# Weight sums of the last product moved from the MLP's first half to the three output projections

## The chip, the cores and the metric

One core of a Trainium2 chip runs the whole kernel. The metric is device time in microseconds (us) of one execution. Three runs of the kernel before gave 1279.53, 1282.16 and 1282.68 us, so the median is 1282.16 us. One further execution was profiled: it took 1281.15 us, of which 1279.1 us lie between its first and its last instruction. Less than 0.3% (3.8 us) is not told from no change here.

## The reference

The reference is one layer of an encoder over two sequences, a prompt of 512 rows and a sample of 256 rows, each with 16 shared meta rows in front. All data are float32, the width is 1024. Cut to its steps:

```
u    = rms(h);  q, kv, k_rot, conv_in, gates = split(u @ w_in)
attn = latent_attention(q, kv, k_rot) @ w_o_attn                  # 8 heads
c    = depthwise_conv31(glu(conv_in)) + b
c    = silu(layernorm(c));  conv = c @ w_conv_out
h    = h + (sig(gA) * attn + sig(gC) * conv) @ w_out
h    = h + square(relu(rms(h) @ w_mlp_in)) @ w_mlp_out            # hidden width 4096
y    = rms(h)[:, 16:]
```

## The kernel before

**Products.** Each float32 product is made of three TensorE products on a high and a low part of each operand (`products`, L359): high by high, high by low, low by high. The high part is a rounded copy (`hi_unit`, L319, always on ScalarE), the low part is the difference between the weights and their high part (`lo_unit`, L324). A *unit* is 128x1024 weights: it lands in one of four `raw` slots, is split into one of two `whi` and one of two `wlo` slots, and is used by 48 matmuls (36 in the token-major `w_out`, L1850). The split of unit n+2 starts when TensorE has finished unit n. In most of the first part VectorE makes the low parts, because GpSimd ("POOL") has other work later; in the three output projections (`w_o_attn`, `w_conv_out`, `w_out`, eight units each) and in the MLP's first half GpSimd makes nearly all of them.

**Seven products instead of eight.** The last product, hidden by `w_mlp_out`, is done as a two by two block product with seven block products (a Strassen form). It needs sums and differences of the four blocks of `w_mlp_out`. They are made once by the kernel: for each of eight parts j, ScalarE issues two loads of 1 MB into a staging slot (`load_sums`, L841), VectorE makes four subtractions of 128x1024 elements in place (`weight_sums`, L1289 to L1295), and ScalarE issues two stores of 1 MB to a scratch tensor `wsum` in HBM (`store_sums`, L846). There are three staging slots; the list `W_SLOT` says which part uses which. The seven products read `wsum` back much later. Before the change, parts 0 and 1 are loaded at the start of `w_out`, part 2 in the middle of it, and parts 3 to 7 are handled in the MLP's first half.

**The stage around the change.** Every engine has its own list of instructions, written out by hand and run strictly in order; semaphores tie them together. TensorE's list for the three output projections is: eight units of `w_o_attn`, eight of `w_conv_out`, four units of `w_out` for the left half of the columns, four for the right half. Between them stand small products with a matrix of ones: after the first unit the column sums for the LayerNorm's mean (L1810), and after unit 4 of `w_o_attn` those for its variance (L1821). For the variance ScalarE squares eight centred tiles (`ln_squares`, L798) and GpSimd adds the squares up one after the other into `lnacc` (`ln_sq_add`, L1525 and L1528), between its low parts of weights. TensorE waits at L1821 until all eight are added, and what follows in its list waits behind it.

In the loop over the eight units m of `w_conv_out`, VectorE multiplies unit m's result with its gate (`gconv`, L1257), adds it to `zacc` (L1260), and after ScalarE's rounded copy `zhi` (L825) makes the low part `zlo` (L1262). ScalarE's list has, for each m, the high part of the weights of unit m+1 and then `zhi` of m. So the weights' high part of unit m+2 stands behind `zhi` of m, and that waits for VectorE's addition of m.

During the right half of `w_out`, TensorE transposes the new rows of `h` (L1857) for the MLP. The first four transposed tiles share one accumulator, so each waits until VectorE has made the low part of the tile before it (`u2_lo`, L1282), and that waits for ScalarE's high part (`u2_hi`, L836). SyncE ("SP") issues the loads of weights (L407, L486), gates (`gin`, L478) and the rows of x into `h1` (L496).

The two lines that make one part's first difference wait and run are:

```
dve.wait_ge(wst_landed[j], 32)
nc.vector.tensor_tensor(out=b11, in0=b12, in1=b11, op=ALU.subtract).then_inc(wst_made, 1)
```

Of the kernel before, what the change touches and what calls it, by code (L numbers as in the profile page):

```python
# [32 lines left out]
F32 = mybir.dt.float32  # L33
# [6 lines left out]
P = 128  # L40
D = 1024
# [49 lines left out]
W_SLOT = (2, 0, 0, 0, 1, 0, 1, 0)  # L91
# [42 lines left out]
def build(nc, t):  # L134
    with ExitStack() as ctx:
# [83 lines left out]
        gconv = at("gconv", [P, TQ], F32, Z0 + 134912)  # L219
# [17 lines left out]
        wst = [[at(f"wst{e}{g}", [P, 2, D], F32, Z0 + o + 8192 * g) for g in range(2)] for e, o in enumerate((90112, 73728, 151552))]  # L237
# [161 lines left out]
        def _(sp):  # L399
# [91 lines left out]
            for g in range(2 * KD + 3):  # L491
                m = g % KD
                if g == 2 * KD:
                    sp.wait_ge(c_lo, KD)
                    for e, (name, t0, nt) in enumerate((("x_prompt", 0, 4), ("x_sample", 4, 2))):
                        sp.dma_start(h1[:, t0:t0 + nt], t[name][0].rearrange("(t p) n -> p t n", p=P)) \  # L496
                          .then_inc(h_landed[e], 16)
# [42 lines left out]
        def _(act):  # L540
# [245 lines left out]

            for h in range(EARLY_HEADS, HEADS):
# [20 lines left out]
            hi_unit(act, U_O, 1, 3)  # L808
            for k in range(KD):
# [27 lines left out]
            wm = t["w_mlp_out"][0].rearrange("(g u k p) n -> g p u k n", g=2, k=2, p=P)  # L837

            def load_sums(j):
                for g in range(2):  # L840
                    act.dma_start(wst[W_SLOT[j]][g][:, :, :], wm[g, :, j]).then_inc(wst_landed[j], 16)  # L841

            def store_sums(j):
                act.wait_ge(wst_made, 4 * (j + 1))
                for g in range(2):
                    act.dma_start(wsum[g, j], wst[W_SLOT[j]][g][:, :, :]).then_inc(wst_stored[j], 16)  # L846
            act.wait_ge(unit_used, U_OUT)
            load_sums(0)
            act.wait_ge(z_lo, KD)
            load_sums(1)  # L850
            hi_unit(act, U_OUT, 0, 1)
            hi_unit(act, U_OUT, 0, 2)
            store_sums(0)
            hi_unit(act, U_OUT, 0, 3)
            store_sums(1)
            hi_unit(act, U_OUT, 0, 4)
            act.wait_ge(wst_stored[1], 32)
            load_sums(2)
            for i in range(NT):
                h_square(0, i)  # L860
            hi_unit(act, U_OUT, 0, 5)
            hi_unit(act, U_OUT, 0, 6)
            act.wait_ge(wst_stored[0], 32)
            store_sums(2)
# [28 lines left out]
            def in_step(i):  # L893
                for c in range(4):
# [54 lines left out]
        def _(dve):  # L949
# [268 lines left out]

            def gate_attn(m):
# [22 lines left out]
            gate_attn(2), gate_attn(3), gate_attn(4)  # L1242
# [11 lines left out]
            for m in range(KD):  # L1254
                dve.wait_ge(unit_used, U_CO + m + 1)
# [24 lines left out]
            def u2_lo(k):  # L1280
                dve.wait_ge(u2hi_ready, k + 1)
                nc.vector.scalar_tensor_tensor(out=u2lo[:, k], in0=psum[:, U2_PAIR[k], 0:TQ], scalar=vcol("norm_mlp", k),  # L1282
                                               in1=u2hi[:, k].bitcast(F32), op0=ALU.mult, op1=ALU.subtract).then_inc(u2lo_ready, 1)
            def weight_sums(j):

                a, b = wst[W_SLOT[j]]
                b11, b12, b21, b22 = a[:, :, 0:HALF], a[:, :, HALF:D], b[:, :, 0:HALF], b[:, :, HALF:D]
                dve.wait_ge(wst_landed[j], 32)
                nc.vector.tensor_tensor(out=b11, in0=b12, in1=b11, op=ALU.subtract).then_inc(wst_made, 1)  # L1289
                dve.wait_ge(wst_made, 4 * j + 1)  # L1290
                nc.vector.tensor_tensor(out=b12, in0=b22, in1=b12, op=ALU.subtract).then_inc(wst_made, 1)
                dve.wait_ge(wst_made, 4 * j + 2)
                nc.vector.tensor_tensor(out=b22, in0=b22, in1=b11, op=ALU.subtract).then_inc(wst_made, 1)
                dve.wait_ge(wst_made, 4 * j + 3)
                nc.vector.tensor_tensor(out=b21, in0=b22, in1=b21, op=ALU.subtract).then_inc(wst_made, 1)  # L1295

            weight_sums(0), weight_sums(1)
            h_add(0)
            weight_sums(2)
# [45 lines left out]
            def in_step(i):  # L1345
                for c in range(4):
# [3 lines left out]
                    if f == KH:  # L1350
                        for j in range(3, PU):
                            dve.wait_ge(wst_stored[j], 32)
# [6 lines left out]
                    if f in (2, 4, 6, 9, 12):  # L1359
                        weight_sums((2, 4, 6, 9, 12).index(f) + 3)  # L1360
# [82 lines left out]
        def _(gp):  # L1443
# [92 lines left out]
            for n in range(U_O + KD, U_IN + 1):  # L1536
# [435 lines left out]
```

## Time and profile before

| | us |
|---|---|
| median of three runs | 1282.16 |
| profiled execution | 1281.15 |
| its span, first to last instruction | 1279.1 |
| TensorE busy with matmuls | 1249.1 |
| VectorE busy | 813.0 |
| ScalarE busy | 486.5 |
| GpSimd busy | 257.0 |
| HBM read, written | 115.32 MB, 26.21 MB |

TensorE's clock was granted in full for 0.996 of the span. A busy share says how full an engine is over all stages; for one stage it has to be read in a window of it. In a list of instructions in order of time, the bracket at a row's end gives the time for which the engine stood idle before that instruction, and what ended that. VectorE's duration of an instruction can contain waiting inside it: the same subtraction of 128x1024 elements shows 1.22 us in some rows and 3.3 us in others.

### The profile page before, as it was taken

To read this page: it belongs to the slowest core of one execution; us is meant where nothing else is said; L and a number is where in the kernel's file an instruction comes from. 1 tells how busy PE (TensorE), PEld (TensorE's weight loads), DVE (VectorE), ACT (ScalarE), POOL (GpSimd) and SP (SyncE) were. 2 spreads that over 40 slices of the span, in tenths; PEclk is the share of its full clock that TensorE was granted. 3 is DMA by queue.
4 is the path that set the end of the run, shared out by engine and by line. 5 is a ranking of instruction groups with operands and counts; after the bars stand their busy time and mean duration, and the time that the engine had idled before them with its cause. 6 is when DMAs were issued, how large, how long until landed. Compare 5 with 4: busy or idle time off the path is not lost.

```text
span 1279.1 us, 17675 instructions
## 1 busy us (share of the span) xinstructions
PE 1249.1 (98%) x7037; PEld 1086.7 (85%) x7037; DVE 813.0 (64%) x966; ACT 486.5 (38%) x731; POOL 257.0 (20%) x172
## 2 busy tenths in 40 slices
PE   6999999999999999989999989999999999999997
PEld 4888888888889999978888878888888888888886
DVE  4699999998867777764833533645111146678865
ACT  6211122532156676753621224221222244444452
POOL 2000000000034344347322322323333210000001
PEclk9999999999999999999999999999999999999999
DMA  6222222333220011114353935665312234333332
GB/s 188 67 66 66 57 67 66 104 111 107 90 66 22 22 42 33 34 30 144 100 203 109 361 141 181 237 224 201 124 55 63 66 111 149 131 126 126 131 132 98
DMA packets 136693, 142.36 MB, mean 111 GB/s; under 512 B 10573, under 2 KB 106891, under 8 KB 134586
## 3 DMA queue, kind: packets, MB, share of 16 engines
q1 hardware_dynamic: 127488, 101.55, 26.3%
q10 hardware_dynamic: 9146, 40.01, 8.2%
q8 instruction: 39, 0.64, 0.2%
q14 instruction: 20, 0.16, 0.0%
HBM read 115.32 MB, written 26.21 MB: 111 GB/s over the span
## 4 chain that ended last, share of the span: by engine, by line
PE 88%; DVE 4%; ACT 3%; DMA 2%; issue 2%; ACTq 1%; POOL 0%; POOLq 0%; DVEq 0%
PE psum L359 59%; PE psum L1929 17%; PE psum L1714 4%; PE psum L1746 2%; PE psum L1850 2%; DMA wst<-in_w_mlp_out 2%; PE psum L1726 1%; PE psum L1672 1%; DVE acc L1030 1%; PE psum L1590 1%; PE psum L1555 1%; DMA wsum<-wst 1%; ACT uhi L565 0%; DVE olo L1178 0%; PE psum L1857 0%
## 5 line engine op out<-in xcount | busy, mean ns | idle before, releaser
L324 POOL TENSOR_TENSOR wlo<-raw,whi 128x1024 fp32r<-128x1024 f32 (+2 forms) x70 | 166.6, 2380 | 684.1 <-ACT whi L319 684.1
L1030 DVE SCALAR_TENSOR_TENSOR acc<-cs,convw,acc 128x799 f32<-128x799 f32 x232 | 230.2, 1057 | 0.2
L319 ACT ACTIVATE whi<-raw 128x1024 fp32r<-128x1024 f32 (+1 forms) x113 | 114.0, 1009 | 294.1 <-PE psum L359 253.6
L359 PE MATMUL psum<-uhi,wlo 128*128 128x512 f32 x592 | 152.8, 339 | 0.0
L359 PE MATMUL psum<-uhi,whi 128*128 128x512 f32 x592 | 152.2, 338 | 0.5 <-DVE wlo L324 0.5
L359 PE MATMUL psum<-ulo,whi 128*128 128x512 f32 x592 | 152.5, 338 | 0.0
L1355 DVE SCALAR_TENSOR_TENSOR hid<-psum,rbc 128x768 f32<-128x768 f32 x32 | 30.6, 956 | 174.0 <-PE psum L359 173.9
L359 PE MATMUL psum<-u2hi,whi 128*128 128x512 f32 (+1 forms) x512 | 131.0, 336 | 0.0
L359 PE MATMUL psum<-u2hi,wlo 128*128 128x512 f32 (+1 forms) x512 | 130.6, 336 | 0.0
L359 PE MATMUL psum<-u2lo,whi 128*128 128x512 f32 (+1 forms) x512 | 130.6, 336 | 0.0
L916 ACT ACTIVATE hid<-hid 128x768 f32<-128x768 f32 x32 | 27.1, 846 | 200.5 <-DVE hid L1355 182.8
L359 PEld LDWEIGHTS psum<-uhi,whi 128*128 128x128 f32 x592 | 91.4, 188 | 14.0 <-issue 0.8
L359 PEld LDWEIGHTS psum<-uhi,wlo 128*128 128x128 f32 x592 | 91.6, 188 | 12.9
L359 PEld LDWEIGHTS psum<-ulo,whi 128*128 128x128 f32 x592 | 91.3, 188 | 12.3
L886 ACT ACTIVATE hidhi<-hid 128x768 fp32r<-128x768 f32 x56 | 47.3, 846 | 110.2 <-PE psum L1929 108.9
L359 PEld LDWEIGHTS psum<-u2lo,whi 128*128 128x128 f32 x512 | 78.3, 188 | 10.5
L359 PEld LDWEIGHTS psum<-u2hi,whi 128*128 128x128 f32 x512 | 78.3, 188 | 10.3
L359 PEld LDWEIGHTS psum<-u2hi,wlo 128*128 128x128 f32 x512 | 78.1, 188 | 10.5
L1329 DVE TENSOR_TENSOR hidlo<-hid,hidhi 128x768 fp32r<-128x768 f32 x56 | 53.7, 960 | 50.9 <-ACT hidhi L886 50.9
L324 DVE TENSOR_TENSOR wlo<-raw,whi 128x1024 fp32r<-128x1024 f32 (+1 forms) x39 | 47.1, 1207 | 30.2 <-ACT whi L319 30.2
L1929 PE MATMUL psum<-whi,hidlo 128*128 128x512 f32 x168 | 65.4, 389 | 0.0
L1929 PE MATMUL psum<-wlo,hidhi 128*128 128x512 f32 x168 | 65.4, 389 | 0.0
(243 smaller groups left out, 2512.7 us busy)
## 6 DMA issues: line engine op xcount, KB each, us to landing
raw<-in_w_in SPq DMA_DIRECT2D x38, 512.0 KB, 4.0
wst<-in_w_mlp_out ACTq DMA_DIRECT2D x16, 1024.0 KB, 8.0
wsum<-wst ACTq DMA_DIRECT2D x16, 1024.0 KB, 5.9
raw<-in_w_mlp_in SPq DMA_DIRECT2D x32, 512.0 KB, 4.0
raw<-wsum SPq DMA_DIRECT2D x32, 512.0 KB, 4.1
raw<-in_w_mlp_out SPq DMA_DIRECT2D x24, 512.0 KB, 3.6
gates<-gout ACTq DMA_DIRECT2D x16, 384.0 KB, 2.5
gin<-gates SPq DMA_DIRECT2D x16, 384.0 KB, 3.1
```

What stands on the lines that cost most here:

```text
L319: nc.scalar.activation(whi[:, c % 2, 0:w], raw[:, c % 4, 0:w], ACT.Copy).then_inc(hi_ready, 1)
L324: eng.tensor_tensor(out=wlo[:, c % 2, 0:w], in0=raw[:, c % 4, 0:w], in1=whi[:, c % 2, 0:w].bitcast(F32), op=ALU.subtract).then_inc(lo_read ...
L359: mm = nc.tensor.matmul(out[:, o0:o0 + n], a, b[:, k, c0:c0 + n], start=first and step == 0, stop=last and step == 2)
L886: nc.scalar.activation(hidhi[u % 4][:, :, :], f_block(n, c), ACT.Copy).then_inc(hidhi_ready, 1)
L916: nc.scalar.activation(r, r, ACT.Square).then_inc(hid_ready, 1)
L1030: ins = nc.vector.scalar_tensor_tensor(out=a, in0=src, scalar=w, in1=a, op0=ALU.mult, op1=ALU.add)
L1329: nc.vector.tensor_tensor(out=hidlo[u % 4][:, :, :], in0=f_block(n, c), in1=hidhi[u % 4][:, :, :].bitcast(F32), op=ALU.subtract).then_inc( ...
L1355: nc.vector.scalar_tensor_tensor(out=hid[:, ds(i * 4 + c, 1), :], in0=psum[:, pair:pair + 1, 0:TQ], scalar=0.0, in1=rbc[:, :].rearrange("p ...
L1714: mm = nc.tensor.matmul(psum[:, q % 2, e * HALF:e * HALF + n], a[:, c0:c0 + P], b[:, grp["k0"] + k0:grp["k0"] + k0 + n], start=step == 0, ...
L1746: mm = nc.tensor.matmul(bank[:, 7, 0:2 * P], a[:, vt, hh * VD:(hh + 1) * VD], r[:, blk % 2, e, :], start=e == 0 and step == 0, stop=False)
L1850: mm = nc.tensor.matmul(out, a, b[:, kk, :], start=first and step == 0, stop=last and step == 2)
L1929: mm = nc.tensor.matmul(bank[:, P_BANKS[n % 2][tt]], a, b[:, kk, :], start=c == 0 and kk == 0 and step == 0, stop=c == PU - 1 and kk == 1 ...
```

## The change

All eight parts of the weight sums are made during the three output projections, none in the MLP's first half. There are now five staging places instead of three, in memory that is free at the time, and `W_SLOT` names them anew. Four things move:

1. Parts 0 and 1 are loaded at the end of attention and at the start of `w_o_attn`. VectorE makes part 0 after the gate of unit 2, part 1 after the gate of unit 3; ScalarE stores them before the variance's root. Parts 2 to 5 are loaded in the `w_conv_out` loop at m = 0, 2, 4, 6; VectorE makes parts 2, 3, 4 at m = 1, 3, 6, ahead of `gconv` of that m; ScalarE stores them at m = 2, 4, 7. Parts 6 and 7 are loaded at the start of `w_out`, and parts 5, 6, 7 are made in its first three steps.
2. In the `w_conv_out` loop and for units 0 to 3 of `w_out`, VectorE makes the low parts of the weights; GpSimd goes on from unit 4 of `w_out`.
3. The rows of x are loaded after the eighth unit of `w_conv_out` and after part 4 is stored, no longer in the middle of that loop, because their place is now a staging place. Four loads of `w_out` weights stand behind them in SyncE's list.
4. `gconv` gets other memory, and some waits for stores stand ahead of operations that reuse a staging place.

The core of the diff (new places of the tiles, and the removal of the same calls in the MLP's first half and of the old definition, are left out):

```diff
-W_SLOT = (2, 0, 0, 0, 1, 0, 1, 0)
+W_SLOT = (0, 1, 2, 3, 2, 3, 4, 1)
...
@@ sync
             row_units(wo, U_OUT, 0)(0, [3])
+            sp.wait_ge(c_lo, KD)
+            sp.wait_ge(wst_stored[4], 32)
+            for e, (name, t0, nt) in enumerate((("x_prompt", 0, 4), ("x_sample", 4, 2))):
+                sp.dma_start(h1[:, t0:t0 + nt], t[name][0].rearrange("(t p) n -> p t n", p=P)) \
+                  .then_inc(h_landed[e], 16)
             row_units(wo, U_OUT + 4, 1)(0)
...
@@ scalar
+            act.wait_ge(av_mm, 6 * PAIRS)
+            load_sums(0)
             hi_unit(act, U_O, 0, 2)
...
+            act.wait_ge(o_lo, KD)
+            load_sums(1)
             hi_unit(act, U_O, 0, 3)
...
             ln_squares(range(6, 8))
+            store_sums(0)
             hi_unit(act, U_O, 1, 2)
+            store_sums(1)
             act.wait_ge(var_mm, 1)
...
             for m in range(KD):
                 if m > 0:
                     hi_unit(act, U_CO, m // 4, m % 4 + 1)
+                if m in (2, 4, 7):
+                    store_sums((2, 4, 7).index(m) + 2)
+                if m == 0:
+                    act.wait_ge(c_lo, KD)
+                if m in (4, 6):
+                    act.wait_ge(wst_stored[m // 2], 32)
+                if m in (0, 2, 4, 6):
+                    load_sums(m // 2 + 2)
                 act.wait_ge(merged, KD + m + 1)
                 nc.scalar.activation(zhi[:, m], zacc[:, m], ACT.Copy).then_inc(z_hi, 1)
...
@@ vector
-            gate_attn(2), gate_attn(3), gate_attn(4)
+            gate_attn(2)
+            weight_sums(0)
+            gate_attn(3)
+            weight_sums(1)
+            gate_attn(4)
...
             for m in range(KD):
+                if m == 0:
+                    dve.wait_ge(lo_ready, U_CO + 1)
+                lo_unit(dve, U_CO + (m + 1) // 4 * 4, 0, (m + 1) % 4)
+                if m in (1, 3, 6):
+                    weight_sums((1, 3, 6).index(m) + 2)
                 dve.wait_ge(unit_used, U_CO + m + 1)
...
-            weight_sums(0), weight_sums(1)
+            for c in range(1, 4):
+                lo_unit(dve, U_OUT, 0, c)
+                weight_sums(4 + c)
             h_add(0)
-            weight_sums(2)
             u2_lo(0), u2_lo(1), u2_lo(2), u2_lo(3)
...
@@ gpsimd
-            for n in range(U_O + KD, U_IN + 1):
+            lo_unit(gp, U_CO, 0, 0)
+            gp.wait_ge(lo_ready, U_OUT + 4)
+            for n in range(U_OUT + 4, U_IN + 1):
                 lo_unit(gp, n - n % 4, 0, n % 4)
```

VectorE around the variance, before. `zacc` out of `psum` is the gate of one unit; `lnr` is the reciprocal of the LayerNorm's root.

```order
L1222 TENSOR_TENSOR zacc<-psum,gin 128x768
L1228 TENSOR_TENSOR cs<-cs,mu 128x768 x3
L1222 TENSOR_TENSOR zacc<-psum,gin 128x768 x3
L1245 RECIPROCAL lnr<-lnacc 128x768
L1222 TENSOR_TENSOR zacc<-psum,gin 128x768
```

The same stretch of VectorE in the changed kernel (its lines are numbered some 20 higher); `wst_140` to `wst_143` are the staging tiles of parts 0 and 1.

```order
L1239 TENSOR_TENSOR zacc<-psum,gin 128x768
L1227 TENSOR_TENSOR wst_140<-wst_140 128x2x512
L1229 TENSOR_TENSOR wst_140<-wst_141,wst_140 128x2x512
L1232 TENSOR_TENSOR wst_141<-wst_141,wst_140 128x2x512
L1234 TENSOR_TENSOR wst_141<-wst_141 128x2x512
L1239 TENSOR_TENSOR zacc<-psum,gin 128x768
L1227 TENSOR_TENSOR wst_142<-wst_142 128x2x512
L1229 TENSOR_TENSOR wst_142<-wst_143,wst_142 128x2x512
L1232 TENSOR_TENSOR wst_143<-wst_143,wst_142 128x2x512
L1234 TENSOR_TENSOR wst_143<-wst_143 128x2x512
L1239 TENSOR_TENSOR zacc<-psum,gin 128x768
L1268 RECIPROCAL lnr<-lnacc 128x768
```

Eight subtractions now stand between the gates of units 2, 3 and 4. GpSimd's list is the same in this stretch in both kernels:

```order
L324 TENSOR_TENSOR wlo<-raw,whi 128x1024
L1528 TENSOR_TENSOR lnacc<-lnacc,lnsq 128x768 x3
L324 TENSOR_TENSOR wlo<-raw,whi 128x1024
L1528 TENSOR_TENSOR lnacc<-lnacc,lnsq 128x768 x2
```

None of these six rows moved; they now run beside VectorE's new ones. Next, ScalarE in the `w_conv_out` loop, before:

```order
L825 ACTIVATE zhi<-zacc 128x768
L319 ACTIVATE whi<-raw 128x1024
L825 ACTIVATE zhi<-zacc 128x768
L319 ACTIVATE whi<-raw 128x1024
L825 ACTIVATE zhi<-zacc 128x768
L319 ACTIVATE whi<-raw 128x1024
```

And in the changed kernel, from m = 1 to m = 3:

```order
L850 ACTIVATE zhi<-zacc 128x768
L319 ACTIVATE whi<-raw 128x1024
L796 DMA wsum<-wst_144 128x2048
L796 DMA wsum<-wst_145 128x2048
L791 DMA wst_146<-in_w_mlp_out 128x2x1024
L791 DMA wst_147<-in_w_mlp_out 128x2x1024
L850 ACTIVATE zhi<-zacc 128x768
L319 ACTIVATE whi<-raw 128x1024
L850 ACTIVATE zhi<-zacc 128x768
```

Part 2 is stored and part 3 is loaded in one go at m = 2. VectorE in the same loop of the changed kernel, from the end of m = 2 through m = 3 (before, only `gconv`, `zacc`, `zlo` follow each other):

```order
L1290 TENSOR_TENSOR zlo<-zacc,zhi 128x768
L324 TENSOR_TENSOR wlo<-raw,whi 128x1024
L1227 TENSOR_TENSOR wst_146<-wst_146 128x2x512
L1229 TENSOR_TENSOR wst_146<-wst_147,wst_146 128x2x512
L1232 TENSOR_TENSOR wst_147<-wst_147,wst_146 128x2x512
L1234 TENSOR_TENSOR wst_147<-wst_147 128x2x512
L1285 TENSOR_TENSOR gconv<-psum,gin 128x768
L1288 TENSOR_TENSOR zacc<-zacc,gconv 128x768
L1290 TENSOR_TENSOR zlo<-zacc,zhi 128x768
L324 TENSOR_TENSOR wlo<-raw,whi 128x1024
```

The part that was loaded at m = 2 stands ahead of `gconv` of m = 3, and the low part of unit 5's weights behind `zlo` of m = 3.

## Rows read from the trace of the kernel before

**Rows 1.** The page's first part: busy time of each engine.

```profile
PE 1249.1 (98%) x7037; PEld 1086.7 (85%) x7037; DVE 813.0 (64%) x966; ACT 486.5 (38%) x731; POOL 257.0 (20%) x172
```

**Rows 2.** Waits of TensorE: who for whom, total us, times, longest us.

```profile
PE psum L1555 <- DVE xt L956: 10.5, 2, 10.3
...
PE psum L1857 <- DVE u2lo L1282: 3.9, 1, 3.9
...
PE psum L1850 <- POOL wlo L324: 0.3, 1, 0.3
```

**Rows 3.** Busy us per engine by window, then clock share, DMA share, GB/s.

```profile
744.00:748.00 4.00, 1.46 (x7) 0.88 (x5) 2.38 (x1) 0.66 (x1) 1.30 (x1) 1.00 0.31 79
748.00:752.00 4.00, 2.65 (x10) 2.36 (x11) 1.16 (x2) 1.14 (x2) 0.00 (x0) 0.65 1.06 427
752.00:756.00 4.00, 4.00 (x19) 3.27 (x18) 0.88 (x1) 0.04 (x1) 0.00 (x0) 0.93 0.36 150
...
820.00:840.00 20.00, 20.00 (x117) 17.66 (x116) 12.95 (x13) 5.39 (x6) 6.90 (x3) 1.00 0.72 263
...
920.00:940.00 20.00, 20.00 (x117) 17.62 (x116) 2.50 (x4) 5.39 (x6) 6.24 (x3) 1.00 0.18 52
```

**Rows 4.** In order of time, VectorE and ScalarE, 743 to 749 us.

```profile
743.08 3.30 DVE L1295 TENSOR_TENSOR wst<-wst 128x1024 f32<-128x1024 f32 x1
...
747.34 0.90 ACT L836 ACTIVATE u2hi<-psum,vec 128x768 fp32r<-128x768 f32 x1 [5.49 <-DVE wst L1295]
...
748.28 1.02 DVE L1282 SCALAR_TENSOR_TENSOR u2lo<-psum,vec,u2hi 128x768 fp32r<-128x768 f32 x1 [1.90 <-ACT u2hi L836]
```

**Rows 5.** In order of time, GpSimd, 591 to 606 us.

```profile
591.61 2.41 POOL L324 TENSOR_TENSOR wlo<-raw,whi 128x1024 fp32r<-128x1024 f32 x1
593.97 5.85 POOL L1528 TENSOR_TENSOR lnacc<-lnacc,lnsq 128x768 f32<-128x768 f32 x3
599.78 2.41 POOL L324 TENSOR_TENSOR wlo<-raw,whi 128x1024 fp32r<-128x1024 f32 x1
602.14 3.85 POOL L1528 TENSOR_TENSOR lnacc<-lnacc,lnsq 128x768 f32<-128x768 f32 x2
```

**Rows 6.** In order of time, TensorE at the variance's column sums.

```profile
605.95 0.51 PE L359 MATMUL psum<-ohi,wlo 128*128 128x512 f32 x2
606.29 1.45 PE L1821 MATMUL psum<-lnacc,ones 128*128 128x512 f32 x4
```

**Rows 7.** VectorE and GpSimd beside each other, three places.

```profile
583.27 3.16 DVE L1228 TENSOR_TENSOR cs<-cs,mu 128x768 f32<-128x768 f32 x1
...
598.17 0.96 DVE L1222 TENSOR_TENSOR zacc<-psum,gin 128x768 f32<-128x768 f32 x1 [7.36 <-PE psum L359]
...
805.45 3.23 POOL L324 TENSOR_TENSOR wlo<-raw,whi 128x1024 fp32r<-128x1024 f32 x1 [5.92 <-ACT whi L319]
...
806.43 3.32 DVE L1293 TENSOR_TENSOR wst<-wst,wst 128x1024 f32<-128x1024 f32 x1
```

**Rows 8.** In order of time, the `w_conv_out` loop, VectorE and ScalarE.

```profile
637.31 1.56 DVE L1237 TENSOR_TENSOR clo<-cs,chi 128x768 fp32r<-128x768 f32 x1 [0.83 <-ACT chi L814]
...
649.39 0.96 DVE L1257 TENSOR_TENSOR gconv<-psum,gin 128x768 f32<-128x768 f32 x1 [4.50 <-PE psum L359]
...
652.12 1.04 ACT L319 ACTIVATE whi<-raw 128x1024 fp32r<-128x1024 f32 x1
...
652.25 0.96 DVE L1262 TENSOR_TENSOR zlo<-zacc,zhi 128x768 fp32r<-128x768 f32 x1 [0.91 <-ACT zhi L825]
...
657.71 0.96 DVE L1257 TENSOR_TENSOR gconv<-psum,gin 128x768 f32<-128x768 f32 x1 [4.50 <-PE psum L359]
```

**Rows 9.** DMA issues, KB each, median us to landing: all, then those at 845 us.

```profile
wst<-in_w_mlp_out ACTq DMA_DIRECT2D x16, 1024.0 KB, 8.0
...
845.17 2.29 ACTq L841 DMA_DIRECT2D wst<-in_w_mlp_out  x2
...
wst<-in_w_mlp_out ACTq DMA_DIRECT2D x2, 1024.0 KB, 10.4
```

More of the change, by code:

```diff
@@ L218, in build @@
         lnacc = at("lnacc", [P, TQ], F32, Z0 + 147200)
-        gconv = at("gconv", [P, TQ], F32, Z0 + 134912)
+        gconv = at("gconv", [P, TQ], F32, Z0 + 33024)
         zhi = at("zhi", [P, KD, TQ], F32R, Z0 + 36096)
@@ L236, in build @@
         junk2 = at("junk2", [P, HALF], F32, Z0 + 167936)
-        wst = [[at(f"wst{e}{g}", [P, 2, D], F32, Z0 + o + 8192 * g) for g in range(2)] for e, o in enumerate((90112, 73728, 151552))]
+        wst = [[at(f"wst{e}{g}", [P, 2, D], F32, Z0 + o + 8192 * g) for g in range(2)] for e, o in enumerate((110336, 151552, 0, 134912, 90112))]
         wsum = nc.dram_tensor("wsum", [2, PU, P, 2, D], F32, kind="Internal").ap()
@@ L492, in _ @@
                 m = g % KD
[L493 to L497, printed above, removed]
                 if g >= 2 * KD:
@@ L784, in _, with load_sums, store_sums @@
             rolled(act, PAIRS, pair_step, peel=1, last=1)
+            wm = t["w_mlp_out"][0].rearrange("(g u k p) n -> g p u k n", g=2, k=2, p=P)
+            def load_sums(j):
+                for g in range(2):
+                    act.dma_start(wst[W_SLOT[j]][g][:, :, :], wm[g, :, j]).then_inc(wst_landed[j], 16)
+            def store_sums(j):
+                act.wait_ge(wst_made, 4 * (j + 1))
+                for g in range(2):
+                    act.dma_start(wsum[g, j], wst[W_SLOT[j]][g][:, :, :]).then_inc(wst_stored[j], 16)
             for h in range(EARLY_HEADS, HEADS):
                 o_split_hi(h)
+            act.wait_ge(av_mm, 6 * PAIRS)
+            load_sums(0)
             hi_unit(act, U_O, 0, 2)
@@ L808, in _ @@
             hi_unit(act, U_O, 1, 3)
+            act.wait_ge(wst_stored[0], 32)
             for k in range(KD):
@@ L836, in u2_hi @@
                 nc.scalar.activation(u2hi[:, k], psum[:, U2_PAIR[k], 0:TQ], ACT.Copy, scale=vcol("norm_mlp", k)).then_inc(u2hi_ready, 1)
[L837 to L846, printed above, removed]
+            hi_unit(act, U_OUT, 0, 1)
+            act.wait_ge(z_lo, KD)
+            load_sums(6)
             act.wait_ge(unit_used, U_OUT)
[L848 to L851, printed above, removed]
+            load_sums(7)
             hi_unit(act, U_OUT, 0, 2)
-            store_sums(0)
+            store_sums(5)
             hi_unit(act, U_OUT, 0, 3)
-            store_sums(1)
+            store_sums(6)
             hi_unit(act, U_OUT, 0, 4)
-            act.wait_ge(wst_stored[1], 32)
-            load_sums(2)
+            store_sums(7)
+            hi_unit(act, U_OUT, 0, 5)
             for i in range(NT):
                 h_square(0, i)
-            hi_unit(act, U_OUT, 0, 5)
             hi_unit(act, U_OUT, 0, 6)
-            act.wait_ge(wst_stored[0], 32)
-            store_sums(2)
+            act.wait_ge(wst_stored[5], 32)
             u2_hi(0), u2_hi(1)
@@ L1217, in _, with weight_sums @@
             combine(LAST, KD * TAPS)
+            def weight_sums(j, parts=(0, 1)):
+                a, b = wst[W_SLOT[j]]
+                b11, b12, b21, b22 = a[:, :, 0:HALF], a[:, :, HALF:D], b[:, :, 0:HALF], b[:, :, HALF:D]
+                if 0 in parts:
+                    dve.wait_ge(wst_landed[j], 32)
+                    nc.vector.tensor_tensor(out=b11, in0=b12, in1=b11, op=ALU.subtract).then_inc(wst_made, 1)
+                    dve.wait_ge(wst_made, 4 * j + 1)
+                    nc.vector.tensor_tensor(out=b12, in0=b22, in1=b12, op=ALU.subtract).then_inc(wst_made, 1)
+                if 1 in parts:
+                    dve.wait_ge(wst_made, 4 * j + 2)
+                    nc.vector.tensor_tensor(out=b22, in0=b22, in1=b11, op=ALU.subtract).then_inc(wst_made, 1)
+                    dve.wait_ge(wst_made, 4 * j + 3)
+                    nc.vector.tensor_tensor(out=b21, in0=b22, in1=b21, op=ALU.subtract).then_inc(wst_made, 1)
             def gate_attn(m):
@@ L1281, in u2_lo @@
                 dve.wait_ge(u2hi_ready, k + 1)
+                if k == 0:
+                    dve.wait_ge(wst_stored[7], 32)
                 nc.vector.scalar_tensor_tensor(out=u2lo[:, k], in0=psum[:, U2_PAIR[k], 0:TQ], scalar=vcol("norm_mlp", k),
                                                in1=u2hi[:, k].bitcast(F32), op0=ALU.mult, op1=ALU.subtract).then_inc(u2lo_ready, 1)
[L1284 to L1295, printed above, removed]
-            weight_sums(0), weight_sums(1)
+            for c in range(1, 4):
+                lo_unit(dve, U_OUT, 0, c)
+                weight_sums(4 + c)
             h_add(0)
-            weight_sums(2)
             u2_lo(0), u2_lo(1), u2_lo(2), u2_lo(3)
@@ L1349, in in_step @@
                         x_lo(0), x_lo(1), f_lo(1)
-                    if f == KH:
-                        for j in range(3, PU):
-                            dve.wait_ge(wst_stored[j], 32)
+                    if f == 0:
+                        dve.wait_ge(wst_stored[6], 32)
                     dve.wait_ge(unit_used, i * 4 + (U_IN + c + 1))
```

15 lines of the change are left out of this document (2 added, 13 removed).

## The prediction

> **What bounds the kernel now.** I read the page's first part, then TensorE's waits, then windows over the stages that the change touches, then lists of instructions in order of time.
>
> TensorE is busy with matmuls for 98% of the span [rows 1]. So a microsecond counts only where TensorE stands still or runs at a lower clock. Its waits [rows 2] show three that matter here: 10.5 us at the very start, which the change does not touch; one wait of 3.9 us in `w_out` for `u2lo`; and 0.3 us for a low part of weights in `w_out`. The MLP's first half, where parts 3 to 7 are made now, has nothing to give: TensorE is busy for 20.00 us of 20 and shows 117 matmuls both in a window with weight sums (VectorE 12.95 us busy) and in one without (2.50 us) [rows 3]. What the change takes away from that stage is therefore worth 0.
>
> The wait in `w_out` comes from the weight sums: ScalarE idles 5.49 us until VectorE's last subtraction of part 2, which runs from 743.08 to 746.38, then makes `u2hi` at 747.34, and VectorE makes `u2lo` at 748.28 [rows 4]. After that wait TensorE shows a granted clock of 0.65 and then 0.93 in two windows of 4 us [rows 3], which is part of the time at 1.2 GHz instead of 2.4 GHz. The loss is (1 - 0.65) x 4 + (1 - 0.93) x 4 = 1.7 us. I charge 1.7 us for each wait of TensorE of about 4 us or more.
>
> **What goes away.** In the changed kernel no store or subtraction stands between ScalarE's high parts and `u2hi` 0, and the sums are past before the right half starts. 3.9 + 1.7 = 5.6 us. The 0.3 us for a low part goes too, since the two loads that delayed ScalarE there now stand behind that high part, and VectorE makes the low part. Together -5.9 us. What is late next is the transposed tile itself, and that follows TensorE's own pace, so nothing takes the wait's place.
>
> **Added in `w_o_attn`: eight subtractions beside GpSimd's chain of squares.** GpSimd is busy without a gap from 591.61 to 605.99: low part, three additions, low part, two additions [rows 5]. The variance's column sums start on TensorE at 606.29, directly behind the last product of the unit [rows 6]. GpSimd's chain has 0.3 us to spare.
>
> The two engines hinder each other. A subtraction that takes 1.22 us alone took 3.32 us from 806.43, where GpSimd's low part ran from 805.45 to 808.68; it ended at 809.75, 1.07 us after GpSimd did. GpSimd's own row took 3.23 us where 2.41 is usual [rows 5, 7]. The row at 583.27 shows the same with the operation `centre` [rows 7]. The gate at 598.17 took its usual 0.96 us in the middle of GpSimd's additions [rows 5, 7]: its first input lies in PSUM. So what has both inputs in SBUF takes turns with GpSimd, what reads PSUM does not.
>
> The gate of unit 2 ends at about 590.8, eight us before that of unit 3. Part 0 starts there; part 1 follows the gate of unit 3. Taken in turns: the four subtractions of part 0 come ahead of the low part and the three additions; the gate of unit 3 runs beside one addition; three subtractions of part 1 come ahead of the second low part and the last two additions. Seven of eight subtractions delay the chain. Behind a low part the cycle is 3.23 - 0.95 + 1.07 = 3.35 us (0.95 us of the 3.23 are the wait for the subtraction before), in place of 2.36 from start to start: +1.0. Behind an addition (1.95 from start to start, of which about 0.1 is a gap that the turn swallows, and as much of its start-up) it is +0.83. Sum 2 x 1.0 + 5 x 0.83 = 6.1 us, less 0.3 to spare: 5.8 us of wait on TensorE, and 1.7 us of clock: **+7.5 us**. The bounds are 0 (if the turns fell in gaps) and 7 x 1.22 + 1.7 = 10.2. A gain is excluded: nothing there gets less. What stands behind the wait is TensorE's unit 5 and all that follows; VectorE's reciprocal and the scaling shift with it and keep their distance, and ScalarE's store of part 1, ahead of the root, costs it some 0.8 us that the reciprocal has to spare.
>
> The Trainium skill speaks against this place, in "SBUF — State Buffer", section "Who interferes with whom": a VectorE instruction with two SBUF inputs and a GpSimd instruction that reads SBUF exclude each other for the whole instruction of whoever came first. The trace agrees with 3.32 us. By its whole-instruction rule each turn would cost the full 1.22 us, the wait would be 8.2 us, the term 9.9 and the time 1291.1; by the rows above it is 7.5, and I keep that.
>
> **Added in the `w_conv_out` loop.** I count on the clock of before. A subtraction with its start costs 1.25 us, a part 5.0. `gconv` of m = 1 starts at 649.39, that of m = 2 at 657.71, so one unit is 8.32 us, m = 3 is at 666.03 and m = 4 at 674.35 [rows 8]; TensorE starts the next unit 0.2 us ahead of each. From `gconv` of m to the weights' high part of m + 2 it is 652.12 + 1.04 - 649.39 = 3.8 us, and to the end of `zlo` 3.8 us too. The low part on VectorE adds 1.22: 5.0 us from `gconv` of m until unit m + 2 can start. The rule: `gconv` of m may be late by 8.1 - 5.0 = 3.1 us. GpSimd is idle here, since its low parts moved away, so no turns are taken; the low part itself is earlier than on GpSimd (1.22 for 2.4).
>
> Part 2: the last `clo` ends at 638.9 [rows 8], the load lands 8.0 us after issue [rows 9], at 647.0. VectorE subtracts until 652.0; `gconv` of m = 1 is 2.6 us late, within 3.1. No wait, with 0.5 us left.
>
> Part 3: ScalarE reaches its store of part 2 at 652.0 + 3.8 = 655.8 and the load of part 3 at 656.6. Such a load right behind such a store is in the trace at 845.17: the two issues took 2.29 us, and each took 10.4 us to land [rows 9]. The second is therefore down between 667.0 and 668.9; I take 668.3. The subtractions end at 673.3, where `gconv` of m = 3 was due at 666.03. Unit 5's low part is ready at 678.3, and TensorE was ready at 674.1: 4.2 us of wait, and 1.7 us of clock, **+5.9 us**. The bounds: with a landing after 8.0 us it is ready at 674.6, a wait of 0.5; with 668.9, 4.8 + 1.7 = 6.5.
>
> Parts 4 and 5 follow an iteration without sums; part 4 is loaded at m = 4 and subtracted at m = 6, over 12 us later. They cost nothing by this count.
>
> **Added in `w_out`.** A unit is some 8.2 us and the load of part 6 is issued 4 us into the first. With up to 13 us for it (two loads of 2 MB in a row), the subtractions, then unit 3's low part are done 23.2 us in, and it is needed at 24.5. I take 0; the cover is 1.3 us. The x rows (3.1 MB) are moved into the same stretch; they are needed when the first tile of unit 3 is done, some 3 x 8.2 + 1.4 = 26 us in. Four loads of weights behind them in SyncE's list are first needed at 24.5.
>
> **Sum.** -5.9 + 7.5 + 5.9 = +7.5 us. The profiled execution took 1281.15 us (span 1279.1 and 2.05 around it): 1288.7 us. Its distance to the median of before, 1282.16, is 1.0 us; by that a median could read 1 us higher.
>
> **The rivals.**
> - *Only the variance is hit.* The load of part 3 lands after 8 us or is not behind the store. For: the median of all such loads [rows 9]. Against: the one at 845 has just this neighbour. -5.9 + 7.5 = +1.6: 1282.8 us.
> - *Only unit 5 is hit*, since the turns fall in GpSimd's gaps. Against: there are none [rows 5]. 0: 1281.2 us.
> - *Neither: faster.* The sums are hidden and only the wait for `u2lo` goes. It decides whether VectorE's subtractions really push GpSimd's chain. 1275.3 us.
> - *The loads are late everywhere: slower still.* With 10.4 us for part 2, unit 3 waits 1.9 us; in `w_out`, half of the x rows ahead of part 6 (3.7 us at the 427 GB/s of rows 3) leaves unit 3 late by 2.4 us, with some clock. About +5.5 on top: 1294.2 us.
>
> On this last one the Trainium skill, "DMA: Bandwidth & Descriptors", section "Queues, rings and completion order", says that an engine takes its queues in turns, packet by packet. By that the x rows on SyncE's queue would take half the rate from ScalarE's loads, for it, not against it; no row here shows the two side by side.
>
> **How the numbers follow.** Forecast (both places) 0.50, with its own range 1285.5 to 1292; only the variance 0.15; only unit 5 0.08; neither 0.14; late everywhere 0.13. A change under 0.3%, 3.8 us, is not told from none. Faster than 1278.3 is the fourth case and a little of the others: 0.15. Within are the second and third and the low edge of the forecast: 0.24. Slower than 1286.0: 0.61. The range leaves out most of "neither" and the upper part of the last: 1277 to 1295.
>
> **What would show it.** Right: a wait of TensorE at the `lnacc` column sums for GpSimd's last addition, of 4 to 8 us, with subtractions of about 3 us on VectorE beside it; a wait at unit 5 of `w_conv_out` for VectorE's low part; no wait at the transposes. Wrong: `lnacc` ready when TensorE comes, or the load of part 3 down before 664.5 on the clock of before, or any new wait in `w_out`.

## The result, and the profile after

| | before | changed |
|---|---|---|
| median, us | 1282.42 | 1291.54 |
| lowest to highest | 1279.53 to 1283.51 | 1291.35 to 1293.73 |
| executions | 6 | 6 |

The changed kernel is slower by 9.1 us: ratio 1.0079, 95% interval 1.0066 to 1.0092. The forecast was 1288.7 us, 7.5 us over the profiled execution of before. The profiled execution of the changed kernel has a span of 1289.6 us, 10.5 us more than before.

Each experiment below was run in a set together with the kernel before, and its ratio is to that set. The median of before is 1282.42 us here, and 1281.42, 1281.49 and 1282.2 us in the later sets. A difference of medians across two sets is therefore uncertain by about 1 us; "against its own set" means the difference to before in the same set.

The page's first part, changed kernel, against [rows 1]:

```profile
PE 1252.1 (97%) x7037; PEld 1085.5 (84%) x7037; DVE 820.7 (64%) x977; ACT 486.3 (38%) x731; POOL 232.4 (18%) x161
```

TensorE does the same matmuls. Its waits, changed kernel, against [rows 2] (who for whom, total, times, longest):

```profile
PE psum L1572 <- DVE xt L958: 9.0, 2, 8.8
...
PE psum L359 <- DVE wlo L324: 6.1, 2, 5.6
PE psum L1838 <- POOL lnacc L1543: 5.8, 1, 5.8
...
PE psum L1867 <- DVE wlo L324: 0.8, 1, 0.8
```

The wait for `u2lo` is gone. Three are new: 5.8 us at the variance's column sums, 5.6 us at a unit of `w_conv_out` for a low part, and 0.8 us in `w_out`. The first is seen on three engines, in order of time; here VectorE:

```profile
587.33 0.96 DVE L1239 TENSOR_TENSOR zacc<-psum,gin 128x768 f32<-128x768 f32 x1 [1.93 <-PE psum L359]
588.21 1.99 DVE L1227 TENSOR_TENSOR wst<-wst 128x1024 f32<-128x1024 f32 x1
590.23 3.31 DVE L1229 TENSOR_TENSOR wst<-wst,wst 128x1024 f32<-128x1024 f32 x1
593.58 2.76 DVE L1232 TENSOR_TENSOR wst<-wst,wst 128x1024 f32<-128x1024 f32 x1
596.37 2.76 DVE L1234 TENSOR_TENSOR wst<-wst 128x1024 f32<-128x1024 f32 x1
599.05 0.94 DVE L1239 TENSOR_TENSOR zacc<-psum,gin 128x768 f32<-128x768 f32 x1
```

GpSimd in the same stretch, then TensorE, against [rows 5, 6]:

```profile
589.07 3.39 POOL L324 TENSOR_TENSOR wlo<-raw,whi 128x1024 fp32r<-128x1024 f32 x1
592.42 8.42 POOL L1543 TENSOR_TENSOR lnacc<-lnacc,lnsq 128x768 f32<-128x768 f32 x3
600.79 3.38 POOL L324 TENSOR_TENSOR wlo<-raw,whi 128x1024 fp32r<-128x1024 f32 x1
604.14 5.52 POOL L1543 TENSOR_TENSOR lnacc<-lnacc,lnsq 128x768 f32<-128x768 f32 x2
...
609.71 2.93 PE L1838 MATMUL psum<-lnacc,ones 128*128 128x512 f32 x4 [5.78 <-POOL lnacc L1543]
```

The two engines step in time with each other: a subtraction beside an addition takes 2.76 us, and three additions take 8.42 us where they took 5.85. The gate at 599.05, with an input in PSUM, keeps its 0.94 us. The chain from 589.07 to 609.66 takes 20.6 us instead of 14.4. The four matmuls behind it take 2.93 us instead of 1.45: they run at half clock.

The clock by windows, changed kernel, in the columns of [rows 3]: behind the first wait, then behind the second.

```profile
604.00:608.00 4.00, 0.00 (x0) 0.00 (x0) 3.96 (x2) 1.06 (x1) 3.86 (x3) 1.00 1.00 360
608.00:612.00 4.00, 2.29 (x3) 1.18 (x4) 3.57 (x2) 0.39 (x1) 4.00 (x2) 0.64 0.56 183
612.00:616.00 4.00, 4.00 (x13) 3.40 (x12) 2.16 (x1) 1.80 (x2) 0.95 (x1) 0.51 1.02 371
684.00:688.00 4.00, 0.36 (x1) 0.39 (x2) 3.09 (x4) 1.79 (x2) 0.00 (x0) 0.52 0.66 148
688.00:692.00 4.00, 4.00 (x16) 3.38 (x16) 3.06 (x4) 1.79 (x2) 0.00 (x0) 0.62 1.01 423
```

The share is a mean over the window. A share of 0.64 over 4 us, where only the levels 1.0 and 0.5 occur, is 2.9 us at half clock; 0.51 is 3.9 us. (By the same reading the 0.996 given for the whole span before is a mean too: 0.8% of the span was at half clock, not 0.4%.) Together 6.8 us behind the first wait (6.9 behind the second), where [rows 3] have 3.4 us.

The second wait, in order of time: ScalarE's queue at m = 2 of the `w_conv_out` loop, then VectorE.

```profile
661.39 0.83 ACTq L796 DMA_DIRECT2D wsum<-wst  x2
...
662.25 2.46 ACTq L791 DMA_DIRECT2D wst<-in_w_mlp_out  x2
...
677.55 1.23 DVE L1227 TENSOR_TENSOR wst<-wst 128x1024 f32<-128x1024 f32 x1 [7.43 <-DMA wst<-in_w_mlp_out]
```

VectorE can start on part 3 only 15.3 us after the first of its two loads was issued behind the store of part 2. The profile's own figure, the median from issue to landing, is 13.3 us for these two loads, 10.4 for the two at 845 before, and for all 16 loads 11.5 us here and 8.0 before [rows 9]. In `w_out` part 6 is late too: its load is issued at 718.73, and VectorE starts 15.2 us later. The first `u2lo` starts at 759.38 and no matmul waits for it, where [rows 4] have it 3.9 us late:

```profile
733.91 1.22 DVE L1227 TENSOR_TENSOR wst<-wst 128x1024 f32<-128x1024 f32 x1 [7.94 <-DMA wst<-in_w_mlp_out]
...
759.38 1.02 DVE L1312 SCALAR_TENSOR_TENSOR u2lo<-psum,vec,u2hi 128x768 fp32r<-128x768 f32 x1 [7.44 <-DMA wsum<-wst]
```

**Where 10.5 us of span went.** From the gate of unit 2 to that of unit 5 of `w_o_attn` the distance grew from 26.3 to 35.4 us: +9.1. From there to the last `gconv` and the middle of `w_out` another +9.5: 5.6 us of wait with 1.8 of clock, 0.8 us in `w_out`, and about 1.3 us, which is a slower pace of the matmuls (told of at the end) less the 0.3 us of wait that went. From the middle of `w_out` to the transposes' end the distance shrank by 5.65, the `u2lo` wait and its clock. And 2.5 us were won before the changed stage begins, most of it in the first wait for x (8.8 us instead of 10.3). No edit touches that wait, and it lasts 8.7 to 8.9 us in the profiles of all the experiments too, those on the kernel before among them: the 10.3 us belong to the one execution of before that was profiled. 9.1 + 9.5 - 5.65 - 2.5 = 10.45.

### The profile page after: what moved, and what is told of

Same layout as the page of the kernel before. It is cut to its first block, busy times and chain, and to the rows that moved or that the text cites. A ratio compares the mean times of both kernels' runs of the same rounds, so it can differ in the third digit from the quotient of the medians.

```text
span 1289.6 us, 17678 instructions
## 1 busy us (share of the span) xinstructions
PE 1252.1 (97%) x7037; PEld 1085.5 (84%) x7037; DVE 820.7 (64%) x977; ACT 486.3 (38%) x731; POOL 232.4 (18%) x161
## 4 chain that ended last, share of the span: by engine, by line
PE 83%; DVE 5%; ACT 3%; issue 3%; DMA 3%; POOL 2%; ACTq 0%; POOLq 0%; DVEq 0%
PE psum L359 52%; PE psum L1946 16%; PE psum L1731 4%; PE psum L1867 3%; DMA wst<-in_w_mlp_out 3%; PE psum L1763 2%; POOL lnacc L1543 1%; PE psum L1743 1%; PE psum L1689 1%; PE psum L1607 1%; DVE acc L1032 1%; PE psum L1572 1%; ACT whi L319 1%; ACT uhi L565 0%; DVE cs L1249 0%
## 5 line engine op out<-in xcount | busy, mean ns | idle before, releaser
L324 POOL TENSOR_TENSOR wlo<-raw,whi 128x1024 fp32r<-128x1024 f32 (+2 forms) x59 | 137.8, 2336 | 719.2 <-ACT whi L319 719.2
L324 DVE TENSOR_TENSOR wlo<-raw,whi 128x1024 fp32r<-128x1024 f32 (+1 forms) x50 | 60.5, 1210 | 30.2 <-ACT whi L319 30.2
L1946 PE MATMUL psum<-whi,hidhi 128*128 128x512 f32 x168 | 65.4, 389 | 0.0
## 6 DMA issues: line engine op xcount, KB each, us to landing
wst<-in_w_mlp_out ACTq DMA_DIRECT2D x16, 1024.0 KB, 11.5
```

What stands on the lines that cost most here:

```text
L324: eng.tensor_tensor(out=wlo[:, c % 2, 0:w], in0=raw[:, c % 4, 0:w], in1=whi[:, c % 2, 0:w].bitcast(F32), op=ALU.subtract).then_inc(lo_read ...
L1946: mm = nc.tensor.matmul(bank[:, P_BANKS[n % 2][tt]], a, b[:, kk, :], start=c == 0 and kk == 0 and step == 0, stop=c == PU - 1 and kk == 1 ...
```

## The experiments

### The variance's place alone

Kernel extra8 is the kernel before with eight subtractions of the same size at the same place on VectorE, on tiles that nobody else uses, and no load or store. Two memsets fill these tiles once, ahead of the gate of unit 2. Kernel extra4 has only the first four.

```diff
...
-            gate_attn(2), gate_attn(3), gate_attn(4)
+            def extra(n0):
+                for n in range(n0, n0 + 4):
+                    dve.wait_ge(extra_made, n + 2)
+                    nc.vector.tensor_tensor(out=spare[n % 2][:, :, :], in0=spare[(n + 1) % 2][:, :, :], in1=spare[n % 2][:, :, :],
+                                            op=ALU.subtract).then_inc(extra_made, 1)
+            for e in range(2):
+                nc.vector.memset(spare[e][:, :, :], 1.0).then_inc(extra_made, 1)
+            gate_attn(2)
+            extra(0)
+            gate_attn(3)
+            extra(4)
+            gate_attn(4)
...
```

> The kernel before, with nothing of the change but eight added subtractions of 128x1024 elements on VectorE (four after the gate of unit 2 of w_o_attn, four after that of unit 3), both inputs in SBUF, on two spare tiles. No load, no store, no other move. Theory (VectorE and GpSimd take turns, GpSimd's chain of squares has no slack): GpSimd's low part rows there grow from 2.41 to 3.4 us, its additions from 1.95 to 2.8, TensorE waits 5.8 us for lnacc at the variance's column sums, then loses some 3.2 us at the lower clock, as in the changed kernel, and up to 1.5 us in slightly slower units: +9.0 to +10.5 us. Rival (the wait in the changed kernel came from the loads and stores beside the chain, that is from DMA traffic): no wait at lnacc, 0 us.

> As extra8, with only the first four subtractions, after the gate of unit 2. Theory of turns: one turn ahead of a low part (+1.0 us) and three ahead of additions (+0.83 each), less 0.3 us of slack: a wait of 3.2 us for lnacc, and some 1.7 us of clock: +4.9 us. Rival (a fixed cost of a VectorE that is busy when the chain starts, not one per instruction): the same +9 us as extra8, or none.

Measured, against a median of 1281.42 us for the kernel before: extra8 1289.84 us (ratio 1.0059, 1.0043 to 1.0076), extra4 1286.69 us (1.0035, 1.0024 to 1.0047). That is +8.4 us, below the 9.0 to 10.5 expected, and +5.3 us where 4.9 was expected. Waits of TensorE in extra8, then in extra4:

```profile
PE psum L1834 <- POOL lnacc L1541: 5.8, 1, 5.8
PE psum L1870 <- DVE u2lo L1295: 5.2, 1, 5.2
```

```profile
PE psum L1869 <- DVE u2lo L1294: 4.2, 1, 4.2
PE psum L1833 <- POOL lnacc L1540: 3.1, 1, 3.1
```

Eight subtractions without any transfer give the very wait of the changed kernel, four give 3.1 us. That the loads and stores play no part in this wait is shown. The +8.4 us are not the price of this wait alone: in the profile of extra8, 8.0 us come between the gates of units 1 and 5 of `w_o_attn`, 2.1 us behind them, with the wait for `u2lo` at 5.2 us instead of 3.9, and 1.4 us less lie ahead of the stage. extra4's windows, in the columns of [rows 3]:

```profile
604.00:608.00 4.00, 0.92 (x5) 0.57 (x4) 0.96 (x1) 2.34 (x2) 3.86 (x3) 0.97 0.66 173
608.00:612.00 4.00, 4.00 (x11) 2.60 (x12) 0.36 (x1) 0.90 (x1) 1.99 (x1) 0.60 0.34 110
```

That is (0.03 + 0.40) x 4 / 0.5 = 3.4 us at half clock and 1.7 us lost, as in [rows 3].

### Is it the SBUF input?

Kernel psum01 is the changed kernel, and the subtractions of parts 0 and 1 read their first input in PSUM. What lies there is not `w_mlp_out`, so these two parts of the sums, and with them the kernel's output, are not those of the reference; only its time is used.

```diff
+                in0 = (lambda x: psum[:, 2].rearrange("p (k n) -> p k n", k=2)) if j < 2 else (lambda x: x)
...
-                    nc.vector.tensor_tensor(out=b11, in0=b12, in1=b11, op=ALU.subtract).then_inc(wst_made, 1)
+                    nc.vector.tensor_tensor(out=b11, in0=in0(b12), in1=b11, op=ALU.subtract).then_inc(wst_made, 1)
...
```

> The changed kernel, but the eight subtractions of parts 0 and 1 take their first input from PSUM instead of SBUF; parts 0 and 1 of the weight sums are therefore not those of the reference, all else is the same: as many instructions of the same size at the same places, the same loads and stores. Theory of turns (only two SBUF inputs clash): subtractions of about 1.2 us each, no wait at lnacc, 5.8 + 3.2 us and some of the slower units come back: 9.0 to 10 us less than the changed kernel, so about 1282 us, -0.5 to +0.5 us against before. Rival (VectorE's time or the DMA beside it): the wait at lnacc stays, 1291.5 us.

Measured: 1283.18 us (ratio to before 1.0009, 0.9999 to 1.0018). That is 8.4 us under the changed kernel across the sets; against its own set it is +1.8 us where the changed kernel has +9.1, a saving of 7.4 us. The expected 9.0 to 10 us were too much by either count; two other waits grew (unit 5 to 6.0 us, `w_out` to 1.1). GpSimd and VectorE, in order of time:

```profile
591.71 1.22 DVE L1233 TENSOR_TENSOR wst<-psum,wst 128x1024 f32<-128x1024 f32 x1
...
592.46 5.87 POOL L1544 TENSOR_TENSOR lnacc<-lnacc,lnsq 128x768 f32<-128x768 f32 x3
...
592.97 1.22 DVE L1235 TENSOR_TENSOR wst<-psum,wst 128x1024 f32<-128x1024 f32 x1
```

The number, the size and the place of the subtractions are the same, and so are the stores. With one input in PSUM they take 1.22 us, GpSimd's additions take their old 5.87, and no wait for `lnacc` is left. From the gate of unit 2 to that of unit 5 it is 26.3 us again.

The Trainium skill, "SBUF — State Buffer", section "Who interferes with whom", names this exclusion, and this case bears out that part: two SBUF inputs hinder, one does not. The price that the prediction drew from its whole-instruction rule is not what the rows show: an addition's cycle grew from 1.95 to 2.79 us, by 0.84 and not by 1.22. The rows do not show for how much of an instruction its port is held.

### The load of part 3

Kernel load3 is the changed kernel with this load issued at m = 1.

```diff
-                if m in (0, 2, 4, 6):
-                    load_sums(m // 2 + 2)
+                if m in (0, 1, 4, 6):
+                    load_sums({0: 2, 1: 3, 4: 4, 6: 5}[m])
```

> The changed kernel, but ScalarE issues the load of part 3 at m = 1 of the w_conv_out loop instead of m = 2, so ahead of the store of part 2 instead of behind it. Theory (part 3 comes late because its load runs behind that store): the load is down some 10 us earlier, before gconv of m = 2; no wait of TensorE at unit 5 (5.6 us) and no lower clock after it (1.8 us): 7.0 to 7.9 us less than the changed kernel, about 1284 us. Rival 1 (the 5 us of subtraction ahead of gconv are what makes unit 5 late): a wait of 3 us or more at unit 5 stays. Rival 2 (two loads side by side make part 2 late): a new wait at unit 3 of 1 to 4 us, about 1287 us.

Measured: 1283.46 us (ratio to before 1.0015, 1.0005 to 1.0025), 8.1 us under the changed kernel across the sets and 7.1 us less by the difference to before in each set; 7.0 to 7.9 was expected. VectorE goes from the low part to the sums without a pause:

```profile
666.76 1.23 DVE L324 TENSOR_TENSOR wlo<-raw,whi 128x1024 fp32r<-128x1024 f32 x1
667.91 1.22 DVE L1227 TENSOR_TENSOR wst<-wst 128x1024 f32<-128x1024 f32 x1
```

No wait at unit 5 is left; the 5.8 us for `lnacc` stay, and the wait in `w_out` is 1.1 us instead of 0.8. So the subtractions fit into the loop, and only the landing was late.

Kernel load3_first asks what made it late. The load stays at m = 2 and only goes ahead of the store.

```diff
+                if m == 2:
+                    load_sums(3)
                 if m in (2, 4, 7):
                     store_sums((2, 4, 7).index(m) + 2)
...
-                if m in (0, 2, 4, 6):
+                if m in (0, 4, 6):
                     load_sums(m // 2 + 2)
```

> The changed kernel with the two issues of m = 2 in the w_conv_out loop exchanged: the load of part 3 stands ahead of the store of part 2 instead of behind it; the rest is as it was. Theory: part 3 comes late because 2 MB of the store run ahead of it in the same stretch. Then the load lands some 8 to 9 us after its issue instead of 15.3, about 670 on the changed kernel's clock, VectorE starts the sums 7 us earlier, and the wait at unit 5 (5.6 us with some 2 us of clock) falls to under 1 us: 1291.5 - 7.5 = 1284 us. Rival: the transfers share the rate whichever was issued first, and the load still lands 13 us or more after its issue: a wait at unit 5 of 3.5 us or more stays and the time is 1288 to 1291 us.

Measured: 1286.44 us, from 1283.8 to 1289.53 (ratio to before 1.0042, 1.0027 to 1.0056). ScalarE's queue and VectorE:

```profile
660.59 0.91 ACTq L791 DMA_DIRECT2D wst<-in_w_mlp_out  x2
...
661.54 1.17 ACTq L796 DMA_DIRECT2D wsum<-wst  x2
...
670.32 1.23 DVE L1229 TENSOR_TENSOR wst<-wst 128x1024 f32<-128x1024 f32 x1 [1.16 <-DMA wst<-in_w_mlp_out]
```

In the profiled execution (1283.8 us) VectorE starts 9.7 us after the issue instead of 15.3, and the wait is gone, as expected. By the profile's medians the two loads now land after 7.6 us and the store behind them after 13.5, where the store took 7.2 and the loads behind it 13.3: whichever is issued second is late. The median saved only 5.1 us of the 7.5 expected, and its executions differ by 5.7 us. The exchange gives most, but not reliably. The profiled execution was the fastest of the five and has a mean granted clock of 0.996; the other four have 0.992 and 0.993, the changed kernel 0.990 to 0.993. So part of what they lose is time at half clock; behind which wait, no trace shows.

### Both taken away

Kernel psum01_load3 has both edits.

> The changed kernel with both edits tried apart before: the subtractions of parts 0 and 1 take their first input from PSUM (these two parts of the weight sums hold other numbers, so the output is not the reference's), and the load of part 3 is issued one step earlier. If the two waits are two separate losses, both savings add: 8.4 us and 8.1 us off the 1291.5 us of the changed kernel, 1275.0 us; the sum of terms says the same from the other side, 1282.2 - 5.9 + 1.0 for the short wait left in w_out = 1277. Neither the wait for GpSimd's last addition nor the one for a low part at unit 5 is in the trace. Rival: the first wait gives the load of part 3 or the loads of w_out time, so that without it another wait grows (in w_out from 1 to 4 us or more); then the time is 1279 to 1282 us.

Measured: 1275.65 us (ratio to before 0.9954, 0.994 to 0.9968). The savings add: 1291.54 - 8.4 - 8.1 = 1275.0. Against the kernels before of each set they add as well: 7.4 and 7.1 us are 14.5, and 15.0 us were saved together (from +9.1 to -5.8). What is left of TensorE's new waits:

```profile
PE psum L359 <- DVE wlo L324: 0.9, 2, 0.5
...
PE psum L1868 <- DVE wlo L324: 0.7, 1, 0.7
```

That is the prediction's case "neither", which stood at 1275.3.

### The gain without its price

Kernel part2_mlp is the kernel before with one thing moved. Part 2 leaves `w_out`, and the MLP's first half makes six parts instead of five. Slots and loads follow.

```diff
-W_SLOT = (2, 0, 0, 0, 1, 0, 1, 0)
+W_SLOT = (2, 0, 0, 1, 0, 1, 0, 1)
...
-            store_sums(2)
...
-            weight_sums(2)
...
-                    if f in (2, 4, 6, 9, 12):
-                        weight_sums((2, 4, 6, 9, 12).index(f) + 3)
+                    if f in (1, 3, 6, 8, 11, 13):
+                        weight_sums((1, 3, 6, 8, 11, 13).index(f) + 2)
...
```

> The kernel before with one thing moved: part 2 is made not in w_out's right half but in the MLP's first half, which then makes six parts instead of five (sums at f = 1, 3, 6, 8, 11, 13). Theory: the gain of the change is only the wait for u2lo (3.9 us) with its clock (1.7 us), and the MLP's first half has room for one more part: 1282.2 - 5.6 = 1276.6 us, no wait at the transposes, TensorE busy without a gap in the first half of the MLP. Rival: six parts no longer fit beside the first half: a load of a part is late, or the last store is late for the second half, and TensorE waits there for some 3 to 6 us; then the time is 1279 to 1283 us and the wait is seen at the first half's high parts or at the first products with the sums.

Measured: 1274.15 us (1273.71 to 1275.94), ratio to before 0.9944, 0.993 to 0.9957. It is faster than both kernels. A window of the `w_out` stage, then one of the MLP's first half:

```profile
748.00:752.00 4.00, 4.00 (x22) 3.36 (x21) 1.02 (x1) 1.85 (x2) 2.40 (x1) 1.00 0.00 0
...
820.00:840.00 20.00, 20.00 (x117) 17.46 (x117) 11.07 (x10) 5.39 (x6) 5.96 (x3) 1.00 0.87 316
```

There is no wait at the transposes, and TensorE has no gap beside a sixth part either. Of the 7.3 us, 5.6 are the wait and its clock; the interval (5.5 to 9.0 us) just holds 5.6 alone. The two profiled executions differ by 7.4 us of span, and 1.9 us of that lie before the changed stage, 1.5 of them in the first wait for x, which no edit touches. Whether the other 1.7 us between the medians have the same cause no trace shows.

Kernel part2_mlp_hi adds one exchange on ScalarE in `w_out`.

```diff
+            hi_unit(act, U_OUT, 0, 1)
...
-            hi_unit(act, U_OUT, 0, 1)
```

> The same, and ScalarE makes the high part of unit 1 of w_out ahead of the loads of parts 0 and 1 instead of behind them. Theory: this takes the last wait of 0.3 us for a low part in w_out and nothing else: 0.3 us less than the kernel with part 2 moved alone, which is too little to be told. Rival: the loads of parts 0 and 1 are issued about 1 us later and part 0's subtractions delay what is behind them on VectorE: the same or up to 1 us more, with a new wait in w_out's second unit.

Measured: 1273.79 us (1273.31 to 1275.75), ratio to before 0.9942, 0.9928 to 0.9956. The trace still shows the wait it was to remove:

```profile
PE psum L1853 <- POOL wlo L324: 0.3, 1, 0.3
```

So the 0.3 us do not come from this order of ScalarE. The two medians differ by less than can be told.

## Why the prediction was right

**The removed wait, -5.9 us.** Right. part2_mlp shows that it goes, and psum01_load3, which has the gain and neither price, is 5.8 us under before. The 0.3 us in it were given a wrong reason: the loads ahead of the high part. In the changed kernel the low part is VectorE's, which may be what removed it.

**The MLP's first half, 0.** Right: its windows have TensorE busy for 20.00 of 20 us with five parts, with none, and with six.

**The variance, +7.5 us.** The mechanism was right, and so was the wait: 5.8 us forecast, 5.8 measured, by cycles of 3.35 and 2.8 us against 3.35 and 2.78 worked out. The clock was mis-sized. I charged 1.7 us for any wait of about 4 us or more, from one wait of 3.9. Behind the wait of 5.8 the half clock lasted 6.8 us, not 3.4, and of it 2.29 us in the first window and all in the second fell on matmuls: 2.29 / 2 + (1 - 0.51) x 4 = 3.1 us. The term is 9.1 us in the profile of the changed kernel, 7.6 in that of load3, where the same half clock cost 1.6 us, and by the medians of psum01 8.4 across the sets or 7.4 against its own. So the 7.5 forecast is near the low end of what was measured, and that is partly luck: the clock cost load3 nearly the 1.7 us that I charged, but out of 6.9 us at half clock and not out of 3.4.

**Unit 5, +5.9 us.** Right in place and cause: the load behind the store. The wait was 5.6 us, not 4.2. The step "down at 668.3" took the 10.4 us to landing of the loads behind a store at 845 [rows 9]; here the same figure is 13.3 us. On the clock of before (7.4 us less) the load was issued at 654.9, earlier than the 656.6 that I took, and part 3 was down only at 670.2. That was outside my bounds, which ended at 668.9; one row from another stage was no upper bound. Beside these loads SyncE's queue carries weights and gates, and one load of `w_conv_out` took 13.9 us; no run takes them away, so their part in the 13.3 us stays open. The term is 7.4 us in the profile (with 1.8 of clock, not 1.7), and by load3 8.1 across the sets or 7.1 against its own.

**`w_out`, 0.** Off by 0.8 us, and the prediction had named a new wait in `w_out` as a sign of being wrong. Part 6 came 15.2 us after its issue, not 13, more than the cover of 1.3 us. The x rows were issued 2.2 us ahead of it on SyncE's queue. No run takes them away, so how much of the delay is theirs stays open.

**Sum.** With the two large terms taken against their own sets it is 7.4 + 7.1 + 0.8 - 5.9 = +9.4, and +9.1 was measured between the medians; with the differences across the sets (8.4 and 8.1) it would be +11.4. In the profiles it is 9.1 + 7.4 + 0.8 - 5.9 = +11.4, and the start (-2.5) and the slower pace (1.6), which are no part of the change, make 10.5 of it. The forecast of +7.5 was small by the landing of part 3, the clock behind it and the wait in `w_out`, and in the profiled execution by the clock behind the first wait. Of the rivals, "late everywhere" (1294.2) was right in that loads were later than I took them, but part 2 caused no wait.

## What to carry to other kernels

Work put into the free time of one engine must be priced at what it does to the neighbour: VectorE had room beside GpSimd's chain, but each of its operations with two SBUF inputs lengthened the chain by 0.8 to 1.0 us, and with one input in PSUM by nothing. A wait of TensorE costs more than its length, so taking away waits of 5.8 and 5.6 us gave 15 us. When a stage shows no gap either with or without a piece of work, moving that work out of it buys nothing. Such a stage is the first place to try for more of it, as part2_mlp did with one part.

## What the runs showed of the hardware

**The half clock comes in different lengths, and counts only where it meets matmuls.** It lasted 3.4 us behind waits of 3.9 us ([rows 3]) and of 3.1 and 4.2 us (extra4), and 6.8 or 6.9 us behind waits of 5.8 and 5.6 us and the one of 5.2 us in extra8. The same 5.8 us cost different amounts, by where it began. In the changed kernel it began about when the matmuls came back. In load3 it began inside the wait:

```profile
604.00:608.00 4.00, 0.08 (x1) 0.00 (x0) 3.97 (x2) 1.06 (x1) 3.86 (x3) 0.78 1.06 368
608.00:612.00 4.00, 2.14 (x3) 1.11 (x4) 3.72 (x3) 0.24 (x1) 4.00 (x2) 0.50 0.57 175
612.00:616.00 4.00, 4.00 (x21) 3.38 (x21) 2.02 (x1) 1.94 (x2) 1.09 (x1) 0.86 1.06 387
```

Again 6.9 us in all, but 1.8 us of them lie in the first window with nearly no matmul: 2.14 / 2 + 0.14 x 4 = 1.6 us lost instead of 3.1. The stretch from unit 2 to unit 5 agrees: +7.6 us over before in load3, +8.0 in extra8 (from unit 1, since the memsets hold up the gate of unit 2), +9.1 in the changed kernel.

**Two paces of the same matmuls at full clock.** A unit of `w_conv_out` takes 8.32 us before and 8.48 us in the units of the changed kernel that wait for nothing, about 1.6 us over the stretch. I first tied it to the wait for `lnacc`. All the kernels have 8.32 us ahead of that wait. Behind it the changed kernel, extra4 and load3_first have 8.48 us, but extra8 and load3, with the same wait of 5.8 us, keep 8.32. And psum01_load3 has no such wait, yet goes over to 8.48 us at 656.79, where TensorE waited for 0.42 us. So the long wait does not decide it; what does stays open.
